# Rotating the odd halves ahead of the selection's refinements, and laying ScalarE's counts up to band step 40

## The chip, the cores and the metric

The kernel runs as one program on one core of a Trainium2 chip. The metric is the device time of one execution in microseconds, from a median of several runs. TensorE has two clock levels, 1.2 and 2.4 GHz; the profile prints the granted clock as a share of the higher one.

## What is computed

One post-norm decoder layer on 1024 tokens of width 1024, in float32. The part that matters here is the first: one input projection feeds two head groups. Group A scores all earlier keys with an indexer, keeps the 256 best keys of each query and attends to these; group B attends within a window of 128. After it come memory cross-attention and a squared-ReLU MLP.

```
proj = h @ w_in + b_in
dq, dk, dv, iq, ik, iw, sq, sk, sv = split(proj)
dq, dk, iq, ik, sq, sk = apply_rope(each, cos, sin)
score = sum_heads iw * relu(iq . ik) * idx_scale        # -inf above the diagonal
sel = top_k(score, 256)                                 # per query
o_dsa = softmax(dq . k[sel] / 8) @ v[sel]
o_swa = softmax([sq . sk / 8 within 128 keys, sink]) @ sv
h = layer_norm(ALPHA * h + concat(o_dsa, o_swa) @ w_o)
h = layer_norm(ALPHA * h + memory_cross_attention(h, mem))
h = layer_norm(ALPHA * h + squared_relu_mlp(h))
```

## The kernel before, in words

Every float32 product is made of three fp32r matmuls (high times high, low times high, high times low: lines 872 to 874). Whoever makes an operand therefore rounds it to a high part and subtracts to get a low part.

**Projection and rotation.** TensorE works through 28 halves `v` (14 units `r`, two halves each; `project`), 24 matmuls of 512 columns a half, in two PSUM banks by turns. A half may start when VectorE has read the bank of the half two before. For the even half VectorE does `rope_first` (lines 1689, 1691), for the odd half `rope_second` (1706 to 1716). Then ScalarE rounds both rows (`round_roped`, 1276) and stores them to HBM (`store_roped`), GpSimd makes the low parts (774) and ScalarE stores these too (`store_low`).

**Selection.** The 256th best score of each query is found by bisection over the bits of a float, for the six query tiles 2 to 7 (numbered `c` = 0 to 5). A count is one pass over a tile's scores with a trial value. Narrow tiles are counted on VectorE (`tally`, 1787), in `select_for`, which takes steps of a generator (`select_keys`) until a budget of estimated microseconds is used up. Wide tiles are counted on ScalarE (`count_scores`, 1305, a Sign with an accumulator): four tiles per half beside the halves from v = 18 on (`BESIDE_HALF`), then three tiles (5, 4 and 3, widths 1024, 896 and 768) in 63 late counts, spread evenly over the band steps from `COUNT_FROM` to `COUNT_TO`. For each count VectorE issues a find (1763, waits for the count) and an apply (1771, sets the next trial, for which ScalarE's next count of that tile waits). `set_all` puts these pairs on a list `pending`; each step of `select_for` takes one entry off it, `flush(k)` takes entries off until k are left.

ScalarE's order beside the halves is: four counts of the even half, the stores of the last unit's low parts, four counts of the odd half, then the two roundings and their stores. VectorE's order is that of the loop over `v` in its block (shown in the diff).

**Entry to the band.** Before half 27 ends, ScalarE rounds the memory tokens (`round_mem`, 1339) behind the four counts of half 26; VectorE subtracts (`split_mem`, 1972); TensorE's first memory product waits for that.

**Band.** 40 steps `n`, one for each pair of heads of ten tiles (eight of the window, and the first two of sparse attention, which need no selection). A step has TensorE's scores (926, 927), VectorE's mask (2018), ScalarE's two exponentials (1403), TensorE's transposes (1014), ScalarE's copy of them (1414), TensorE's product with the values (1034). Beside them TensorE does the memory cross-attention's weight products (`memory_product`): per memory head four pieces of key and value products with nothing to copy out but two roundings, then eight absorbed products, each of which ScalarE copies out (`stage_out`, 1376) and stores before TensorE may use the bank again. GpSimd splits their weights (782, 787).

**Sparse attention** of the other six tiles follows (steps 40 to 87). A tile's first mask (2035) stands behind the end of its selection on VectorE (`select_until`). The selection's part for the three wide tiles starts when the last of the 63 counts is applied (`wide_set`).

Lines that the prediction's steps touch:

```
COUNT_FROM, COUNT_TO = 3, 32                                        # 198
lo, hi = (left * (m - COUNT_FROM) // (COUNT_TO - COUNT_FROM) for m in (n, n + 1))
NARROW_EARLY, BUDGET_BAND = 0.9, 2.1
```

Of the kernel before, what the change touches and what calls it, by code (L numbers as in the profile page):

```python
# [123 lines left out]
def index_carried(v):  # L124

    return index_rows(v)[0:3] if v % 2 == 0 else range(0)


def index_own(v):

    return index_rows(v)[len(index_carried(v)):]
# [63 lines left out]
N_EARLY_COUNTS = len(COUNTS)  # L195
COUNTS += [(c, k) for k in range(LAST_EARLY_BIT - 1, -1, -1) for c in WIDE_TILES]
BEFORE = [max((p for p in range(q) if COUNTS[p][0] == COUNTS[q][0]), default=None) for q in range(len(COUNTS))]
COUNT_FROM, COUNT_TO = 3, 32


def counts_beside_rope(v):

    if v < WIDE_HALF:
        return range(0)
    n = len(EARLY_TILES)
    return range(n * (v - WIDE_HALF), n * (v - WIDE_HALF + 1))
# [11 lines left out]
NARROW_EARLY, BUDGET_BAND = 0.9, 2.1  # L218
# [81 lines left out]
def build_layer(nc, a):  # L300
# [6 lines left out]
    with ctx:  # L307
# [1305 lines left out]
        def _(dve):  # L1613
# [62 lines left out]
            def rope_first(r):  # L1676

                n, s = A_ROPE + 2 * r, r % 2
                what, hf = ROPE[r][1:]
                tok = slice(hf * HALF, (hf + 1) * HALF)  # L1680
                b = bias_qk[:, BIAS_COLUMN[what]:BIAS_COLUMN[what] + 1]
                if r == 0:
                    dve.wait_ge(trig_done, 2)
                if r >= 2:

                    dve.wait_ge(qk_stored[s], 64 * (r // 2))
                filled(dve, a_full, n)
                src = ring_a[n % 2][:]
                then(dve.scalar_tensor_tensor(out=roped[s][0][:], in0=src, scalar=b, in1=cos[:, tok],
                                              op0=ALU.add, op1=ALU.mult))  # L1690
                dve.scalar_tensor_tensor(out=roped[s][1][:], in0=src, scalar=b, in1=sin[:, tok],  # L1691
                                         op0=ALU.add, op1=ALU.mult).then_inc(a_free[n % 2], 1)

            def rope_second(r):

                n, s = A_ROPE + 2 * r + 1, r % 2
                what, hf = ROPE[r][1:]
                tok = slice(hf * HALF, (hf + 1) * HALF)
                b = bias_qk[:, BIAS_COLUMN[what] + 1:BIAS_COLUMN[what] + 2]
                filled(dve, a_full, n)  # L1700
                src = ring_a[n % 2][:]
                turned = swa_out if r in ROT_IN_PSUM else rot_part[:]
                if r:

                    dve.wait_ge(rope_done, 2 * r)
                c1 = then(dve.scalar_tensor_tensor(out=turned, in0=src, scalar=b, in1=sin[:, tok],
                                                   op0=ALU.add, op1=ALU.mult))
                dve.wait_ge(dve_step, c1)
                emptied(dve, a_free, n - 1)
                dve.tensor_tensor(roped[s][0][:], roped[s][0][:], turned, ALU.subtract)\  # L1710
                    .then_inc(rope_done, 1)
                dve.wait_ge(rope_done, 2 * r + 1)
                dve.scalar_tensor_tensor(out=turned, in0=src, scalar=b, in1=cos[:, tok],
                                         op0=ALU.add, op1=ALU.mult).then_inc(a_free[n % 2], 1)
                emptied(dve, a_free, n)
                dve.tensor_tensor(roped[s][1][:], roped[s][1][:], turned, ALU.add).then_inc(rope_done, 1)
# [8 lines left out]
            def rotate_and_split(v):  # L1725

                r, h = divmod(v, 2)
                for n in index_own(v):
                    index_sum(n)
                if h == 0:  # L1730
                    rope_first(r)
                    return
                carried = index_carried(v + 1)
                rope_second(r)
                for part in range(2):
                    for n in carried[part:part + 1]:
                        index_sum(n)
                    if r < POOL_SPLIT:
                        split_roped(r, part)
                for n in carried[2:]:  # L1740
                    index_sum(n)

            def index_sum(n):

                i, h = IDX[n]
                width = (i + 1) * P
                dve.wait_ge(relu_done, n + 1)
                src, w = ring_i[n % 3][:, 0:width], v_all[:, i, h:h + 1]
                if h == 0:
                    dve.tensor_scalar(score[i][:], src, w, None, ALU.mult).then_inc(i_free[n % 3], 1)  # L1750
                else:

                    indexed(dve, i_free, n - 1)
                    dve.scalar_tensor_tensor(out=score[i][:], in0=src, scalar=w, in1=score[i][:],  # L1754
                                             op0=ALU.mult, op1=ALU.add).then_inc(i_free[n % 3], 1)
                if h == HEADS - 1:
                    indexed(dve, i_free, n)
                    own = slice(i * P, width)
                    chain(dve.tensor_tensor(score[i][:, own], score[i][:, own], causal[:, P:2 * P], ALU.add))
# [175 lines left out]
            def set_all(counts):  # L1935

                for q in counts:
                    pending.extend(set_counted(q))
# [6 lines left out]
            def select_for(us, carry=False):  # L1945

                credit[0] = us + (credit[0] if carry else 0.0)
                while credit[0] > 0 and len(selected) < NT:
                    cost, tile = next(selection)
                    if cost is None:  # L1950
                        credit[0] = 0.0
                        return
                    credit[0] -= cost
                    if tile is not None:
                        selected.add(tile)
                    if pending:
                        pending.pop(0)()

            def flush(left=0):
                while len(pending) > left:  # L1960
                    pending.pop(0)()
# [101 lines left out]
            for v in range(last_half):  # L2063
                if v - 1 in INDEX_HALVES:
                    prepare(INDEX_HALVES[v - 1] - FIRST_TOPK_TILE)
                if v >= BESIDE_HALF:

                    set_all(counts_beside_rope(v))
                    if v % 2:
                        flush(2)  # L2070
                        select_for(NARROW_EARLY)
                        flush()
                    else:
                        select_for(NARROW_EARLY)
                        flush(2)
                rotate_and_split(v)
                flush()
            split_mem()
# [380 lines left out]
```

## Time and profile before

| | us |
|---|---|
| median of 3 runs | 1544.46 (1541.53 to 1545.77) |
| the profiled execution | 1540.02 |
| its span, first to last instruction | 1538.1 |
| TensorE matmul busy | 1457.1 (95% of the span) |
| VectorE busy | 1092.8 (71%) |
| GpSimd busy | 757.8 (49%) |
| ScalarE busy | 497.8 (32%) |

Shares are means over stages with different limits: the projections end at about 247 us, the band runs from there to about 431 us, sparse attention to about 557 us, then output projection, cross-attention and the MLP, which fill the rest. Times of rows are microseconds from the start of the span. In rows of the timeline the first number is the start, the second the duration; what stands in brackets is how long the engine had been idle before and whose end it had waited for. PE is TensorE, PEld its weight loads, DVE VectorE, ACT ScalarE, POOL GpSimd.

### The profile page before, as it was taken

What the parts mean: (1) busy time and instruction counts of PE and PEld (TensorE: products, weight loads), DVE (VectorE), ACT (ScalarE), POOL (GpSimd) and SP (SyncE); (2) the same over time, 40 slices, a digit from 0 to 9 for tenths busy, and PEclk for the clock granted to TensorE, in tenths of its full rate; (3) what the DMA queues carried; (4) which work ended last, traced back from release to release, by engine and by line L of the source; (5) the groups of instructions that cost most, each with busy time, mean ns of one, the idle gap of its engine ahead of it and who ended that gap; (6) DMA issues with size and microseconds to landing.
All of it is one profiled execution on the core that took longest, in us unless ns stands there. A gap on an engine that the chain in (4) does not pass through costs nothing.

```text
span 1538.1 us, 21058 instructions
## 1 busy us (share of the span) xinstructions
PE 1457.1 (95%) x7552; PEld 1239.0 (81%) x7552; DVE 1092.8 (71%) x2097; ACT 497.8 (32%) x1044; POOL 757.8 (49%) x583
## 2 busy tenths in 40 slices
PE   6999888898999999989999899999999999999997
PEld 6877667788989988778887688888888888888885
DVE  7568978788888422873517768777777777777857
ACT  3025467889676631122201111111111111111111
POOL 5341348566730032144223357867677777777612
PEclk9999999999999999999999999999999999999999
DMA  6446244565520032221011002011111102020202
GB/s 238 135 160 171 83 166 153 173 188 162 175 69 15 1 133 75 94 83 40 18 53 55 28 28 82 28 55 55 55 55 56 55 28 83 28 82 1 82 28 82
DMA packets 61478, 128.98 MB, mean 84 GB/s; under 512 B 6976, under 2 KB 34112, under 8 KB 53696
## 3 DMA queue, kind: packets, MB, share of 16 engines
q1 hardware_dynamic: 44352, 100.37, 19.5%
q10 hardware_dynamic: 17024, 27.27, 5.1%
q8 instruction: 61, 1.00, 0.3%
q14 instruction: 41, 0.34, 0.1%
HBM read 100.35 MB, written 27.26 MB: 83 GB/s over the span
## 4 chain that ended last, share of the span: by engine, by line
PE 76%; DVE 13%; issue 5%; ACT 4%; DMA 1%; POOL 1%; ACTq 1%; SPq 0%; DVEq 0%; POOLq 0%
PE banks L872 21%; PE banks L874 21%; PE banks L873 21%; PE banks L1078 4%; PE banks L926 2%; PE banks L1065 2%; PE banks L927 2%; DVE h_buf L2127 2%; PE banks L1034 1%; PE banks L1087 1%; DVE bn L2113 1%; DVE act_lo L2106 1%; DVE score L1754 1%; ACT unread_early L1305 1%; ACT unread_late L1305 1%
## 5 line engine op out<-in xcount | busy, mean ns | idle before, releaser
L782 POOL TENSOR_SCALAR w_hi<-raw 128x512 fp32r<-128x512 f32 x156 | 105.1, 700 | 427.0 <-PE banks L874 282.0
L2252 DVE TENSOR_TENSOR h_buf<-h_buf,banks 128x512 f32<-128x512 f32 x320 | 202.7, 680 | 13.2 <-PE banks L874 9.7
L787 POOL TENSOR_TENSOR w_lo<-raw,w_hi 128x512 fp32r<-128x512 f32 x156 | 210.3, 1380 | 0.0
L872 PE MATMUL banks<-act_hi,w_hi 128*128 128x512 f32 x512 | 200.0, 391 | 1.6 <-DVE act_lo L2106 1.6
L874 PE MATMUL banks<-act_hi,w_lo 128*128 128x512 f32 x512 | 199.7, 390 | 0.0
L873 PE MATMUL banks<-act_lo,w_hi 128*128 128x512 f32 x512 | 199.7, 390 | 0.0
L872 PE MATMUL banks<-seven_hi,hid_hi 128*128 128x512 f32 x392 | 152.6, 389 | 0.0
L872 PE MATMUL banks<-w_hi,act_hi 128*128 128x512 f32 x384 | 152.6, 397 | 0.0
L874 PE MATMUL banks<-seven_hi,hid_lo 128*128 128x512 f32 x392 | 152.5, 389 | 0.0
L873 PE MATMUL banks<-seven_lo,hid_hi 128*128 128x512 f32 x392 | 152.5, 389 | 0.0
L874 PE MATMUL banks<-w_hi,act_lo 128*128 128x512 f32 x384 | 150.0, 391 | 0.0
L873 PE MATMUL banks<-w_lo,act_hi 128*128 128x512 f32 x384 | 149.9, 390 | 0.0
L2215 DVE TENSOR_TENSOR hidden<-hidden 128x512 f32<-128x512 f32 x56 | 53.9, 964 | 119.9 <-ACT hidden L1545 119.9
L1559 ACT ACTIVATE hid_hi<-hidden_sum 128x512 fp32r<-128x512 f32 x70 | 40.4, 625 | 254.7 <-DVE hidden_sum L2223 254.7
L872 PEld LDWEIGHTS banks<-act_hi,w_hi 128*128 128x128 f32 x512 | 96.5, 188 | 22.1 <-issue 2.0
L873 PEld LDWEIGHTS banks<-act_lo,w_hi 128*128 128x128 f32 x512 | 96.5, 189 | 20.0
L874 PEld LDWEIGHTS banks<-act_hi,w_lo 128*128 128x128 f32 x512 | 96.4, 188 | 20.0
L872 PE MATMUL banks<-x_hi,w_hi 128*128 128x512 f32 x224 | 89.6, 400 | 12.0 <-DVE roped L1691 5.0
L1545 ACT ACTIVATE hidden<-banks 128x512 f32<-128x512 f32 x56 | 33.4, 596 | 199.1 <-PE banks L874 199.1
L926 PE MATMUL banks<-key_hi,q_tile 128*128 128x512 f32 (+3 forms) x240 | 85.4, 364 | 10.1 <-DVE score L1750 7.7
L837 POOL TENSOR_TENSOR seven_lo<-seven_sum,seven_hi 128x1024 fp32r<-128x1024 f32 x35 | 88.0, 2514 | 2.9
L787 POOL TENSOR_TENSOR w_lo<-raw_up,w_hi 128x512 fp32r<-128x512 f32 x56 | 88.7, 1609 | 0.0
(222 smaller groups left out, 3511.8 us busy)
## 6 DMA issues: line engine op xcount, KB each, us to landing
raw<-w_down_dram SPq DMA_DIRECT2D x16, 1024.0 KB, 4.8
raw_up<-w_up_dram SPq DMA_DIRECT2D x14, 1024.0 KB, 4.8
q_tile<-qk_dram SPq DMA_DIRECT2D x176, 64.0 KB, 2.8
qk_dram<-q_hi ACTq DMA_DIRECT2D x28, 256.0 KB, 2.1
qk_dram<-roped ACTq DMA_DIRECT2D x28, 256.0 KB, 2.3
x_raw<-x_t_dram SPq DMA_DIRECT2D x8, 512.0 KB, 8.3
raw<-wk_mem_dram SPq DMA_DIRECT2D x4, 1024.0 KB, 6.3
raw<-wv_mem_dram SPq DMA_DIRECT2D x4, 1024.0 KB, 5.5
```

What stands on the lines that cost most here:

```text
L782: pool.tensor_scalar(w_hi[s][:, col], source[:, col], 1.0, 1.0, ALU.mult, ALU.mult)\
L787: pool.tensor_tensor(w_lo[s][:, col], source[:, col], w_hi[s][:, col].bitcast(F32), ALU.subtract).then_inc(w_ready, 1)
L837: pool.tensor_tensor(seven_lo[s][:], source, seven_hi[s][:].bitcast(F32), ALU.subtract)\
L872: pe.matmul(dst, lh, rh, start=(first and n == 0), stop=False)
L873: pe.matmul(dst, lh, rl, start=False, stop=False)
L874: last = pe.matmul(dst, ll, rh, start=False, stop=(final and n == len(parts) - 1))
L926: pe.matmul(dst[:, lo:hi], q, key_hi[key][:, k0 + lo:k0 + hi], start=True, stop=False)
L1078: mm = pe.matmul(ring_a[m % 2][:, h * HEAD:(h + 1) * HEAD], prob_t[d % 2][:, j * P:(j + 1) * P], v_all[:, j, HEADS:HEADS + HEAD], start=(j ...
L1545: act.activation(hidden[hf, odd][:, j, :], ring_a[n % 2][:], ACT.Relu).then_inc(a_free[n % 2], 1)
L1559: act.activation(hid_hi[x % 2][:, j, :], source, ACT.Copy).then_inc(hidden_rounded, 1)
L2215: dve.tensor_tensor(block, block, block, ALU.mult).then_inc(sq_done, 1)
L2252: ins = dve.tensor_tensor(out, out, ring_m[g % 6][:], ALU.add if way > 0 else ALU.subtract)
```

## The change

In VectorE's loop an odd half from v = 19 on now rotates first (`rotate_and_split`), then takes its counts on the list, refines, and applies all that is left; before it applied three of four counts, refined, applied the rest and then rotated. An even half from v = 18 on rotates right after its refinements, with only as many finds and applies done as the refinements took off the list (two entries); before it applied until two entries were left and then rotated. ScalarE's, TensorE's, GpSimd's and SyncE's orders beside the halves stay. The 63 late counts of ScalarE are laid over band steps 3 to 39 instead of 3 to 31; VectorE's finds and applies for them follow one step behind, as before.

```diff
-COUNT_FROM, COUNT_TO = 3, 32
+COUNT_FROM, COUNT_TO = 3, 40
...
                 if v >= BESIDE_HALF:
 
+                    if v % 2:
+                        rotate_and_split(v)
                     set_all(counts_beside_rope(v))
+                    select_for(NARROW_EARLY)
                     if v % 2:
-                        flush(2)
-                        select_for(NARROW_EARLY)
                         flush()
-                    else:
-                        select_for(NARROW_EARLY)
-                        flush(2)
+                        continue
                 rotate_and_split(v)
                 flush()
             split_mem()
```

## Rows read from the trace of the kernel before

**Rows 1.** Page, part 2: TensorE's busy tenths in 40 slices of 38.45 us.
```profile
PE   6999888898999999989999899999999999999997
```

**Rows 2.** Busy time by stretch, two pairs of halves; columns in the first line.
```profile
core 0: us, PE busy (x) PEld busy (x) DVE busy (x) ACT busy (x) POOL busy (x), PEclk, DMA share, GB/s
205.74:219.35 13.61, 11.41 (x49) 8.85 (x48) 10.56 (x39) 9.16 (x19) 7.21 (x6) 1.00 0.58 174
232.96:246.57 13.61, 11.42 (x49) 8.86 (x48) 10.56 (x39) 9.15 (x19) 7.22 (x6) 1.00 0.43 156
```

**Rows 3.** Timeline, TensorE: first and last restart, last projection matmul, first memory product.
```profile
193.94 0.47 PE L872 MATMUL banks<-x_hi,w_hi 128*128 128x512 f32 x1 [1.60 <-DVE roped L1691]
...
241.27 0.47 PE L872 MATMUL banks<-x_hi,w_hi 128*128 128x512 f32 x1 [1.06 <-DVE banks L1713]
...
246.59 0.39 PE L874 MATMUL banks<-x_hi,w_lo 128*128 128x512 f32 x1
...
251.16 0.39 PE L872 MATMUL banks<-mem_hi,w_hi 128*128 128x256 f32 x1 [2.89 <-DVE mem_lo L1972]
```

**Rows 4.** Timeline, VectorE, one pair of halves (24 and 25).
```profile
232.96 0.74 DVE L1689 SCALAR_TENSOR_TENSOR roped<-banks,bias_qk,cos 128x512 f32<-128x512 f32 x1
...
234.27 0.21 DVE L1763 TENSOR_SCALAR refused<-count,offset 128x1 int32<-128x1 f32 x1
...
236.47 0.21 DVE L1763 TENSOR_SCALAR refused<-count,offset 128x1 int32<-128x1 f32 x1 [0.45 <-ACT unread_early L1305]
...
236.85 0.20 DVE L1763 TENSOR_SCALAR refused<-count 128x1 int32<-128x1 f32 x2
...
238.85 0.76 DVE L1706 SCALAR_TENSOR_TENSOR banks<-banks,bias_qk,sin 128x512 f32<-128x512 f32 x1
...
241.76 0.21 DVE L1763 TENSOR_SCALAR refused<-count 128x1 int32<-128x1 f32 x2
```

**Rows 5.** Timeline, ScalarE: rounding, first count of half 26, memory tokens.
```profile
240.36 0.63 ACT L1276 ACTIVATE q_hi<-roped 128x512 fp32r<-128x512 f32 x1 [3.11 <-DVE roped L1710]
...
242.97 1.15 ACT L1305 ACTIVATE unread_early<-score,trial 128x1024 bf16<-128x1024 f32 x1 [0.46 <-ACT q_hi L1276]
...
246.88 1.90 ACT L1339 ACTIVATE mem_hi<-mem_raw 128x2048 fp32r<-128x2048 f32 x1
```

**Rows 6.** Timeline, VectorE: the low part of the memory tokens.
```profile
248.81 2.29 DVE L1972 TENSOR_TENSOR mem_lo<-mem_raw,mem_hi 128x2048 fp32r<-128x2048 f32 x1 [0.47 <-ACT mem_hi L1339]
```

**Rows 7.** Busy time by stretch, the band; columns as in rows 2.
```profile
262.40:400.60 138.20, 122.36 (x927) 115.78 (x926) 110.90 (x512) 122.25 (x299) 89.23 (x97) 0.98 0.57 176
277.80:301.00 23.20, 18.59 (x119) 16.52 (x118) 15.50 (x75) 19.37 (x47) 10.70 (x13) 0.93 0.54 182
301.00:322.30 21.30, 20.26 (x175) 20.05 (x174) 18.29 (x84) 19.83 (x52) 15.91 (x18) 1.00 0.53 151
402.60:430.60 28.00, 25.60 (x192) 23.75 (x191) 26.92 (x70) 14.68 (x45) 20.28 (x22) 1.00 0.61 190
```

**Rows 8.** Groups by line, ScalarE, 251 to 445 us: busy, mean ns | idle before, releasers.
```profile
L1305 ACT ACTIVATE unread_late<-score,trial 128x1024 bf16<-128x1024 f32 (+2 forms) x63 | 65.1, 1034 | 8.3 <-ACT stage_out L1376 4.6 <-DVE trial L1771 3.8
...
L1414 ACT ACTIVATE band_prob_t<-banks 128x512 f32<-128x512 f32 (+1 forms) x40 | 21.9, 548 | 11.6 <-ACT stage_out L1376 8.8 <-PE banks L1014 1.8 <-PE banks L1034 0.9
L1376 ACT ACTIVATE stage_out<-banks 128x512 f32<-128x512 f32 x32 | 18.7, 586 | 6.8 <-DMA g_dram<-stage_out 3.8 <-PE banks L874 3.0
```

**Rows 9.** Timeline, TensorE: three restarts in the band and after.
```profile
292.42 0.47 PE L872 MATMUL banks<-w_hi,kv_hi 128*128 128x512 f32 x1 [2.64 <-issue]
...
424.33 0.47 PE L872 MATMUL banks<-w_hi,kv_hi 128*128 128x512 f32 x1 [1.39 <-issue]
...
557.62 1.16 PE L1087 MATMUL banks<-ident,h_buf 128*128 128x128 f32 x8 [2.35 <-DVE act_lo L2106]
```

**Rows 10.** Timeline, VectorE: last selection step of tile 5, its first mask.
```profile
465.96 0.56 DVE L1874 TENSOR_SCALAR score<-score 128x768 f32<-128x768 f32 x1
...
475.85 0.96 DVE L2035 CUSTOM_DVE_ANT_0 logit<-banks,score 128x768 f32<-128x768 f32 x1
```

## The prediction

> **What bounds the kernel now.** I read the busy tenths first [rows 1]: TensorE is at nine tenths almost everywhere, at eight in slices 5 to 8 and 10 (about 154 to 308 us and 346 to 385 us). The change touches just these: the end of the projections (up to 247 us) and the sliding-window band (251 to 431 us). So the question is who makes TensorE wait in each, stage by stage.
>
> *The rotation half.* One pair of halves takes 13.61 us, and no engine is busy for all of it [rows 2]: it is a chain. TensorE starts each half late, after VectorE has read the bank of two halves before; there are eight such restarts from 193.94 to 241.27 us [rows 3]. VectorE comes late because it waits for ScalarE: before the odd half it applies three counts (the last find, at 236.47, waited for ScalarE), then runs two refinements from 236.85, and only at 238.85 rotates [rows 4]. ScalarE then has idled 3.11 us for that rotation before it may round it, and starts its next counts 2.61 us later [rows 5]. The circle is: rotate, round, eight counts, find, refine, rotate.
>
> *The entry to the band.* After the last projection matmul (246.59) TensorE scores for a moment and then waits 2.89 us for the low part of the memory tokens [rows 3]. That part starts at 248.81 because ScalarE, late by its counts, rounds the high part only at 246.88 [rows 5, 6].
>
> *The band.* From 262.40 to 400.60 us (steps 3 to 32) TensorE is idle for 138.20 - 122.36 = 15.84 us, and ScalarE is busy for 122.25 [rows 7]. ScalarE also stands still behind its own copies before their store is issued: 8.8 + 4.6 = 13.4 us in the band, for 32 copies [rows 8], so 0.42 each and some 10 for the 24 copies of this stretch. That makes 132 of 138: ScalarE is the bound on average. By phase: while key and value products run (301.00 to 322.30) TensorE is idle for only 1.04 us; while the absorbed products with their copies run (277.80 to 301.00) it idles 4.61 [rows 7], as before 292.42, where the bank had not been copied out [rows 9]. The next idle time of TensorE that the timeline marks after 431 us is the one before 557.62 [rows 9]: sparse attention is bound by TensorE, and what the band gains is not taken back there.
>
> **The change, part by part.** *1. The odd half rotates first, the even half waits for one count only.* Nothing is removed: per pair VectorE still has one first rotation (1.31 us, 232.96 to 234.27), one second (2.91, 238.85 to 241.76), two groups of two refinements with a find and apply inside (2.00 each, 236.85 to 238.85) and six more finds with their applies (0.38 each, 236.47 to 236.85) [rows 4]. Sum 1.31 + 2.91 + 4.00 + 2.28 = 10.50 us. ScalarE has eight counts (four take 242.97 to 246.88, 3.91) and two roundings with their stores (240.36 to 242.97, 2.61) [rows 5]: 7.82 + 2.61 = 10.43. TensorE has 48 matmuls; from 241.27 to 246.59 lie 23 steps of 0.231 [rows 3], so 48 make 11.1, or 11.0 without the two slow starts. So each engine has less than 11.1 us of work per pair, and the order must decide whether they overlap.
>
> I walk one pair from the moment T when TensorE fills the odd bank. VectorE rotates to T+2.9, refines to T+4.9, applies three to T+6.05; the next even group refines to T+8.05 and rotates the first half to T+9.35, then applies three to T+10.5. TensorE fills the next odd bank at T+11.0: VectorE waits for it 0.5. TensorE needs the even bank free by T+11.0 (free at T+9.35) and the odd by T+5.5 (free at about T+2.2). ScalarE rounds the second half at T+2.9, may count from T+4.0, and gets its next trial at T+4.9; four counts end at T+8.8, the other four at T+12.7, which the next odd group asks for only from T+15. Nobody waits for ScalarE any more. The added waits: the even group's first find stands ahead of the first rotation; its count ended about T+6.1 and it is asked for at T+7.1. Stores, GpSimd's split (waiting for the rounding) and the weight splits behind it move along with the pair; GpSimd is idle in half of it [rows 2].
>
> So a pair goes from 13.61 to 11.0. TensorE's eight halves from 193.94 take 44 us instead of the 52.9 up to 246.8, and the first restart, held 1.60 us, comes some 0.7 earlier: **-9.6**. At the entry ScalarE finishes its even counts some 2 us ahead of the last matmul and rounds the memory tokens then; the low part (2.29 us) ends about 2.2 us after TensorE's last projection matmul instead of 4.6: **-2.4**. Together **-12.0**. Bounds: -9 if the entry gives nothing and VectorE's slack of 0.5 is lost in half of the pairs; -13 if TensorE's pair takes 10.9 and the entry gap closes.
>
> *2. Counts up to step 40.* The 63 late counts spread over 37 steps instead of 29: 49 stay in steps 3 to 31, 14 go to steps 32 to 39. A count costs ScalarE 1.034 us [rows 8], so 14.5 us leave the saturated stretch. Lower bound of the gain: only what falls on steps with copies, about half, 7. Upper: all 14.5, as TensorE's idle time is 15.84. I take **-10**, between them: the relief in the other half clears ScalarE's backlog before the copies start, but buffers hold only about a step. In steps 32 to 39 (402.60 to 430.60) ScalarE is busy 14.68 of 28.00 us [rows 7]; with 8 standstills of 0.42 some 10 are free, so 14.5 overrun by 4.5. VectorE is busy 26.92 there and gets 14 times 0.38, 5.3 us, into 1.1 of free time: 4.2 over. Behind a find that waits for a late count stand VectorE's next mask, ScalarE's exponential and TensorE's transposes. The two overruns lie side by side, and exponentials run ahead of TensorE; below, the loss is 0, above, 14.5 if each count pushes a copy that TensorE waits for (as at 424.33 [rows 9]). I take **+5**, the nearer to the overruns. The selection ends its part for tile 5 at 465.96 and is needed at 475.85 [rows 10], 9.9 us of cover; a delay of 5 costs nothing, beyond 10 each us would show. Counts now end at step 40, before the selection asks for them some 10 us later.
>
> **Sum:** -12.0 - 10 + 5 = -17.0 us. The profiled execution took 1540.02 us (span 1538.1), the median of the runs is 4.4 us above it, within their spread. 1540.02 - 17.0 = 1523.0 there; on the median, **1527.5**.
>
> **TensorE's clock** is the one place where a rule would alter the sum. The granted clock was 0.93 from 277.80 to 301.00, where it idled 2.64 us before 292.42, and 1.00 from 301.00 to 322.30 [rows 7, 9]. Over 262.40 to 400.60 it was 0.98: 4% of the time, 5.5 us, at 1.2 instead of 2.4 GHz, 2.8 us of work lost. The Trainium skill, "TensorE: Matmul & The Clock Gate" (HAM oscillation), says that an array which stands idle between bursts is throttled again and begins the next burst slowly; by that the shorter idle times would return these 2.8 us as well and the sum would be -19.8, and the trace agrees so far that the slow matmuls follow the longest idle times.
>
> **Rivals.** *A. The late counts eat what the early ones gave.* The early gain is 7, the late loss 12: -7, **1537**. For: VectorE is full in steps 32 to 39; against: ScalarE has 10 us free there. *B. VectorE or ScalarE becomes the bound of the rotations*, by a second circle through the finds, and a pair falls only half way, to 12.3: -5.2 for the pairs, -1.5 at the entry, -5 in the band: -11.7, **1533**. For: 10.50 and 10.43 us of work lie close below 11.0; against: the walk finds no wait. *C. The clock stays up:* -19.8, **1524.7**. *D. The reordering does not do what it says:* TensorE's pair stays at 13.6, since it is held by something that the walk misses; only -5 from the band, **1539.5**. Against: all eight restarts end with a rotation. *E. Slower.* Steps 35 to 39 have copies, counts, finds and the selection's slow last steps at once: each moved count stands before a copy (14.5) and each find before a mask (5.3), in turn, +19.8, while the early relief gives nothing because masks and not ScalarE held TensorE. -12.0 + 19.8 = +7.8, **1552**. It decides once the late loss is over 16.6 with no early gain. Against: the idle times in the copy phases end with copies.
>
> **How the numbers follow.** Forecast 0.61 (its own range 1519 to 1535), A 0.15, B 0.10, C 0.07, D 0.03, E 0.04. The range 1519 to 1538 takes in the forecast, B, C and most of A. About 0.3%, 4.6 us, can be told from no change. Faster by more: forecast, B, C, most of A and half of D, 0.91; same 0.05; slower 0.04.
>
> **What would show it.** Right: no restart with idle time from the third pair on, pairs of 11.0 us, the last projection matmul near 237 us, the wait for the memory tokens at about 1 us, TensorE's idle time between steps 3 and 32 near 6 us instead of 15.84, and steps 32 to 40 about 5 us longer than the 28 here. Wrong: a pair above 12 us with VectorE waiting for a count; steps 32 to 40 longer by 10 or more; masks waiting for the selection near tile 5.

## The result and the profile after

The changed kernel takes **1530.34 us** (median of 4 runs, 1530.00 to 1532.35), the kernel before, on the same chip, 1543.41 (4 runs, 1541.53 to 1545.77): a ratio of 0.9918, interval 0.9905 to 0.9932, or 13.1 us less. The profiled execution of after took 1530.0 us (span 1528.2); that of before 1540.02, below each of its four runs (the prediction took it to lie within their spread), so the two traces differ by only 9.9 us. The forecast was 1527.5.

I follow six events through both traces. Lead is the time by which after is ahead of before.

| event on TensorE | before | after | lead |
|---|---|---|---|
| last projection matmul | 246.59 | 236.59 | 10.0 |
| first memory product | 251.16 | 239.36 | 11.8 |
| transposes of band unit 26 | 384.99 | 363.10 | 21.9 |
| transposes of band unit 33 | 415.45 | 396.06 | 19.4 |
| transposes of band unit 39 | 433.86 | 420.50 | 13.4 |
| end of attention (second group of transposes of `h_buf`) | 557.62 | 545.45 | 12.2 |

**The rotations.** Two consecutive pairs of after, in the columns of [rows 2]:

```profile
207.36:218.40 11.04, 11.04 (x50) 9.17 (x49) 10.54 (x42) 9.22 (x19) 2.89 (x3) 1.00 0.83 248
218.40:229.44 11.04, 11.04 (x50) 9.13 (x50) 10.39 (x40) 9.29 (x19) 10.24 (x11) 1.00 0.70 238
```

A pair takes 11.04 us instead of 13.61, and TensorE is busy for all of it. Of the eight restarts of [rows 3] one is left, and the wait for the memory tokens is shorter (timeline, TensorE):

```profile
193.19 0.47 PE L872 MATMUL banks<-x_hi,w_hi 128*128 128x512 f32 x1 [0.82 <-DVE roped L1691]
...
236.59 0.39 PE L874 MATMUL banks<-x_hi,w_lo 128*128 128x512 f32 x1
...
239.36 0.39 PE L872 MATMUL banks<-mem_hi,w_hi 128*128 128x256 f32 x1 [1.09 <-DVE mem_lo L1972]
```

VectorE's order in a pair (timeline) shows why: the second rotation now waits for TensorE and for nothing else, where in [rows 4] it stood behind a count and two refinements.

```profile
212.56 0.75 DVE L1689 SCALAR_TENSOR_TENSOR roped<-banks,bias_qk,cos 128x512 f32<-128x512 f32 x1
...
214.62 0.20 DVE L1763 TENSOR_SCALAR refused<-count,offset 128x1 int32<-128x1 f32 x1
...
215.26 0.76 DVE L1706 SCALAR_TENSOR_TENSOR banks<-banks,bias_qk,sin 128x512 f32<-128x512 f32 x1 [0.18 <-PE banks L874]
```

**The band.** Busy time from the mask of unit 3 to that of unit 32, and from there to that of unit 39; columns as in [rows 2]. First before, then after:

```profile
262.38:398.89 136.51, 120.67 (x913) 114.09 (x912) 109.21 (x506) 120.56 (x295) 87.54 (x96) 0.97 0.57 179
398.89:427.04 28.15, 26.42 (x207) 25.11 (x206) 27.18 (x76) 15.30 (x47) 21.82 (x21) 1.00 0.52 160
```

```profile
249.87:379.51 129.64, 118.77 (x917) 113.19 (x916) 103.77 (x480) 108.68 (x269) 90.11 (x101) 0.99 0.61 193
379.51:411.05 31.54, 29.60 (x219) 28.17 (x217) 29.62 (x93) 25.50 (x68) 21.95 (x22) 0.95 0.50 154
```

In the long stretch ScalarE has 11.9 us less to do, and the time falls by 6.9. In the short one ScalarE has 10.2 us more and VectorE 2.4, the time grows by 3.4, and VectorE is busy for 29.62 of 31.54 us. The granted clock there is 0.95, before it was 1.00: TensorE ran a part of these steps at 1.2 instead of 2.4 GHz. Its waits at the end of the band, and the transposes of units 38 and 39 (timeline, TensorE):

```profile
398.39 0.66 PE L1034 MATMUL banks<-v_all,band_prob_t 128*128 128x64 f32 x4 [1.94 <-DVE h_buf L2056]
...
411.97 0.41 PE L926 MATMUL banks<-key_hi,q_tile 128*128 128x384 f32 x1 [0.65 <-DVE neg_max L2018]
...
417.30 1.06 PE L1014 MATMUL banks<-ident,band_prob 128*128 128x128 f32 x4
...
420.50 1.06 PE L1014 MATMUL banks<-ident,band_prob 128*128 128x128 f32 x4
```

The transposes of each of these two units took 1.06 us, in before 0.60: TensorE is at half the clock, behind the waits. Just ahead of them stands a third wait, of 2.51 us before 415.50, for `band_prob_t`; ScalarE has a count and a copy in front of it (timeline, ScalarE):

```profile
412.70 1.03 ACT L1305 ACTIVATE unread_late<-score,trial 128x896 bf16<-128x896 f32 x1
...
413.73 0.57 ACT L1376 ACTIVATE stage_out<-banks 128x512 f32<-128x512 f32 x1
...
414.76 0.60 ACT L1414 ACTIVATE band_prob_t<-banks 128x512 f32<-128x512 f32 x1 [0.46 <-ACT stage_out L1376]
```

**Behind the band** the lead stays near 12 to the end of attention. Then 1.6 us go in the next stage, in which the clock was 0.98 (before: 1.00), although TensorE waited 2.36 us ahead of it in after and 2.35 in before:

```profile
545.45:615.07 69.62, 68.09 (x320) 56.51 (x321) 24.00 (x39) 9.59 (x17) 29.40 (x32) 0.98 0.40 136
```

So: rotations -11.8, counts -7.6 up to unit 33 and +7.2 from there to the end of attention, -12.2 in all; then +1.6 from the clock and 0.7 in small pieces up to the span's 9.9.

### The profile page after: what moved, and what is told of

Read it like the earlier page. It is cut to its first block, busy times and chain, and to the rows that moved or that the text cites. A ratio compares the mean times of both kernels' runs of the same rounds, so it can differ in the third digit from the quotient of the medians.

```text
span 1528.2 us, 21072 instructions
## 1 busy us (share of the span) xinstructions
PE 1458.5 (95%) x7552; PEld 1243.1 (81%) x7552; DVE 1088.0 (71%) x2097; ACT 497.6 (33%) x1044; POOL 756.9 (50%) x583
## 4 chain that ended last, share of the span: by engine, by line
PE 80%; DVE 12%; issue 2%; ACT 2%; DMA 2%; POOL 1%; ACTq 0%; SPq 0%; DVEq 0%; POOLq 0%
PE banks L872 22%; PE banks L874 22%; PE banks L873 22%; PE banks L1078 4%; PE banks L926 2%; PE banks L927 2%; PE banks L1065 2%; DVE h_buf L2126 2%; PE banks L1034 1%; PE banks L1087 1%; DVE bn L2112 1%; DVE act_lo L2105 1%; DMA u_dram<-stage_out 1%; DVE score L1754 1%; DVE h_buf L2135 1%
## 5 line engine op out<-in xcount | busy, mean ns | idle before, releaser
L874 PEld LDWEIGHTS banks<-act_hi,w_lo 128*128 128x128 f32 x512 | 96.6, 189 | 20.1
```

What stands on the lines that cost most here:

```text
L874: last = pe.matmul(dst, ll, rh, start=False, stop=(final and n == len(parts) - 1))
```

## Experiments

In the profiles of kernels that are alike up to there the first memory product comes between 237.4 and 240.7 us, by what lies ahead of the first restart. "Net" therefore means a lead less the lead at the first memory product: what the band itself gained. It still scatters, since each kernel has one profile. In seven profiles whose band is the same up to step 32 (after, counts to 40 only, each half alone, and three rows of the table: less selection late, late counts light, both of these) the net at unit 33 is 3.8 to 8.6, so a difference of 4 us there shows nothing by itself. The loss from unit 33 to 39 is steadier: 5.8 to 6.8 in the four of them that are the same to the end of the band.

| kernel | net at unit 33 | net at unit 39 | median us | ratio to before (interval) |
|---|---|---|---|---|
| after | 7.6 | 1.6 | 1530.3 | 0.9918 (0.9905 to 0.9932) |
| new order only | 1.4 | 1.6 | 1530.0 | 0.9902 (0.9885 to 0.9920) |
| counts to 40 only | 7.2 | 0.4 | 1542.9 | 0.9993 (0.9981 to 1.0005) |
| counts to 35 | 2.3 | -1.4 | 1528.1 | 0.9900 (0.9882 to 0.9917) |
| counts by phase | -7.4 | -11.0 | 1538.2 | 0.9955 (0.9938 to 0.9973) |
| less selection late | 8.6 | 2.8 | 1530.3 | 0.9923 (0.9904 to 0.9943) |
| late counts light | 3.8 | -0.6 | 1531.6 | 0.9930 (0.9909 to 0.9952) |
| both of these | 7.1 | 5.8 | 1525.5 | 0.9899 (0.9873 to 0.9925) |
| counts to 37, less selection late | 6.4 | 6.6 | 1524.1 | 0.9878 (0.9860 to 0.9896) |
| the same, more selection early | 2.8 | 1.8 | 1527.5 | 0.9900 (0.9882 to 0.9918) |
| counts to 32, less selection late | 0.5 | -0.4 | 1531.0 | 0.9911 (0.9891 to 0.9932) |

### Which half carries the circle

The odd half's edit alone (the even half is put back by the added line):

```
                     if v % 2:
                         flush()
                         continue
+                    flush(2)
                 rotate_and_split(v)
```

> After, with the even half put back: it waits again for all but two steps of its finds before the first rotation; the odd half still rotates first. Theory (the circle ran through the odd half's rotation, the even half's wait has slack: the walk found its count ready 1 us ahead): pairs of 11.0 to 11.2 us, the first memory product within 0.5 us of after's 239.36. Rival (both halves carry the circle, each about half): pairs of about 12.3, the first memory product near 244 to 246.

The first restart has 1.59 us of idle time as in before; after it comes no other, and the first memory product is at 240.07, 0.2 us outside the expected 0.5. From restart to memory product it is 46.19 us, in after 46.17, in before 57.22. The one run of this kernel took 1533.1 us.

The even half's edit alone:

```
                     set_all(counts_beside_rope(v))
                     if v % 2:
                         flush(2)
                     select_for(NARROW_EARLY)
                     if v % 2:
                         flush()
                 rotate_and_split(v)
                 flush()
```

> After, with the odd half put back: it applies its counts and runs its refinements ahead of the second rotation; the even half selects first and waits for one count less. Theory: the circle is untouched, pairs of 13.4 to 13.7 us, the first memory product near 250 to 251. Rival (both halves carry the circle): pairs of about 12.3, near 245.

Timeline, TensorE, of this kernel:

```profile
228.67 0.47 PE L872 MATMUL banks<-x_hi,w_hi 128*128 128x512 f32 x1 [2.38 <-DVE banks L1713]
...
242.29 0.47 PE L872 MATMUL banks<-x_hi,w_hi 128*128 128x512 f32 x1 [2.41 <-DVE banks L1713]
...
252.17 0.58 PE L872 MATMUL banks<-mem_hi,w_hi 128*128 128x256 f32 x1 [2.91 <-DVE mem_lo L1972]
```

A pair still takes 13.62 us, and the one run took 1545.6. The two waits of about 1.1 of before have become one of 2.4, at the odd half's rotation. So the odd half's order is the change; the even half's is worth the 0.8 us at the first restart.

### The order alone, the counts alone

```
-COUNT_FROM, COUNT_TO = 3, 40
+COUNT_FROM, COUNT_TO = 3, 32
```

> The new order of the odd and even halves alone; the counts end at step 32 as in the kernel before. Theory (the whole gain of the change is the rotations', the two count terms cancel in the band): 11.8 us less than the kernel before, the saving that the trace of after shows at the first memory product (239.36 against 251.16), so about 1531.6, the time of after. Rival 1 (the prediction's own terms: -12.0, and the longer count range worth -5): 1531.4 here and after about 5 faster. As the terms of the range cannot be told apart by this time alone, the second test is the transposes: by the theory the lead over the kernel before stays near 12 us from step 3 to step 39, by rival 2 (the shorter rotation by itself relieves ScalarE in the band) the lead grows past 15 before step 30 with no late counts at all, and the time falls below 1529.

The lead over before stays between 11.4 and 12.4 us from unit 5 to unit 39. The shorter rotations relieve nobody in the band; rival 2 falls. The time is that of after. It is 14.5 us below before where the traces show 12; the interval reaches down to 12.4, and the clock may have a part in it (below).

The old order with `COUNT_TO = 40`:

> The old order of the halves; the counts run to step 40. Theory (early gain and late loss cancel): within 2 us of the kernel before, 1541.5 to 1545.5; the transposes lead the kernel before by 7 to 10 us around steps 26 to 33 and by less than 3 at the end of the band. Rival (the prediction's terms, -10 early and +5 late, hold by themselves and the loss in after came from a clock that fell there by accident): 1538.4, and the lead at the end of the band is 5.

The lead was 6.1 at unit 26, 5.8 at 33 and -1.0 at 39 (7 to 10 early was expected; the net is 7.2, since its memory product came 1.4 us later than that of before); the interval of the ratio holds 1. **The longer range of counts is worth nothing that the times can tell, by itself or in after.**

### Where the late loss comes from

`COUNT_TO = 35`:

> After, with the counts ended at step 35, ahead of the last head's copies. 14 counts left steps 3 to 31 in after, 6 of 63 leave them here. Theory (the late loss of 7.2 us comes from counts beside copies in steps 35 to 39): early gain 6/14 of the 7.6 to 10 that after had by step 33, so 3 to 4, no late loss: 11.8 + 3.5 less than the kernel before, about 1528, 2 to 3 faster than after. Rival (each count costs its time wherever it stands, the early gain was ScalarE's total and is lost again anyway): the same as after, 1530.5. Third way (counts in steps 32 to 34 already push the copies behind them): slower than after, 1532 or more.

The time, 1528.1, is where the theory put it, but its interval overlaps that of after, and the trace speaks against the theory's reason: of the profile's lead of 14.0 at unit 33 only 10.3 is left at unit 39, though no count is set after step 34. (The profiled execution, 1532.8, was the slowest of its five.) So counts beside the copies of steps 35 to 39 are not the whole of it. In steps 32 to 39 VectorE was busy for 29.35 of 30.41 us.

Next VectorE's selection work was cut there:

```
-select_for(BUDGET_BAND if n < NS else ...
+select_for((BUDGET_BAND if n < 33 else 1.2) if n < NS else ...
```

> After, with VectorE's budget of selection work cut from 2.1 to 1.2 us a step from step 33 on: VectorE gets 7 times 0.9 = 6.3 us less there, which it does later in sparse attention; ScalarE's counts stay. In the run with the new order alone the lead over the kernel before is 12.1 us from the first to the last step, in after it is 19.4 at step 33 and 13.4 at step 39. Theory (VectorE, busy for 29.7 of 31.5 us in steps 32 to 39 of after, is what the late counts overload): the lead stays above 17 to the end of the band, and sparse attention hides the rest, about 1526 or 4 less than after. Rival 1 (ScalarE, busy for 28.6 of 31.5 us there, is what they overload): the lead falls to 13 to 14 as in after and the time is 1530. Rival 2 (the selection is late for its first tiles of sparse attention): the band is shorter and the waits come back behind it as masks, 1530 or more.

```profile
379.77:406.98 27.21, 26.19 (x205) 24.80 (x203) 22.54 (x82) 22.82 (x63) 21.39 (x21) 1.00 0.54 165
...
414.80 0.45 PE L1034 MATMUL banks<-v_all,band_prob_t 128*128 128x64 f32 x1 [3.33 <-ACT band_prob_t L1414]
```

(busy time by stretch, units 32 to 39; timeline, TensorE.) VectorE is free, TensorE's wait for `h_buf` is gone, the clock stays at 1.00, and the lead is 18.5 at unit 37. Then one wait of 3.33 us, behind a count and a copy of ScalarE, and the slower clock behind it (transposes of 1.06 us) take it back to 13.4.

Then ScalarE's part was cut instead:

```
+w = P if q >= len(COUNTS) - 14 else (i + 1) * P
-act.activation(discard[:, 0:(i + 1) * P], score[i][:], ACT.Sign,
+act.activation(discard[:, 0:w], score[i][:, 0:w], ACT.Sign,
```

> After, with the last 14 counts (steps 32 to 39) reading 128 columns instead of the tile's 768 to 1024, which leaves part of these counts out: ScalarE has some 14 times 0.7 = 10 us less there, VectorE's finds stay. Theory (VectorE): the lead over the kernel before still falls from 19 to 13 or 15 in steps 33 to 39, the time within 2 us of after. Rival (ScalarE's counts ahead of the copies): the lead stays near 19 and the time falls to 1525.

```profile
381.26:412.51 31.25, 29.33 (x217) 27.91 (x216) 29.62 (x93) 19.96 (x73) 21.83 (x22) 0.95 0.55 162
...
416.53 0.32 PE L1034 MATMUL banks<-v_all,band_prob_t 128*128 128x64 f32 x1 [2.08 <-DVE h_buf L2057]
```

ScalarE is busy for 19.96 of 31.25 us, 5.5 less than in after, and most of the loss is there all the same (4.4 us from unit 33 to 39, in after 6.0), now with waits that end with VectorE: 1.92 us before 400.11, and the one shown. The light counts took 0.40 us each, and ScalarE stood still before them for 5.3 us in all until VectorE had set their trial values.

Both at once:

> After, with both reliefs of the last steps at once: the last 14 counts read 128 columns (which leaves part of these counts out), and VectorE's budget of selection work is 1.2 us a step from step 33 on. Each relief alone left the lead over the kernel before at 13.2 to 13.4 us at step 39, as in after: in the one run the waits ended with ScalarE's band_prob_t (3.33 us), in the other with VectorE's h_buf (1.92 and 2.08). Theory (ScalarE and VectorE are overloaded side by side, and either alone costs the whole loss): the lead stays at 17 to 19 up to step 39, the time is 1525 to 1527. Rival (a third thing, such as the key and value weights of the last head or the masks of sparse attention, holds the last steps): the lead falls to 13 to 14 again, 1530.

```profile
381.31:408.95 27.64, 25.97 (x205) 24.73 (x203) 22.82 (x82) 17.39 (x65) 21.80 (x21) 1.00 0.53 163
...
414.44 0.29 PE L1034 MATMUL banks<-v_all,band_prob_t 128*128 128x64 f32 x1 [1.97 <-ACT band_prob_t L1415]
```

Of the loss of some 6 us 1.3 is left, and the time falls to 1525.5: its four runs (1524.1 to 1529.9) lie below those of after, though the intervals of the ratios overlap. **VectorE and ScalarE are overloaded side by side, and each alone costs TensorE most of the loss**: relieving one shows nothing in the time. Most of what the double relief saves is not waiting, though. From unit 33 to 39 TensorE was idle for 5.10 us in after, 5.54 and 4.51 with one relief, 3.87 with both, and 2.65 in before; the granted clock of this stretch was 0.84, 0.87, 0.88, then 1.00 with both and in before. Both reliefs take away half of the added waiting and all of the slow clock. The lead at unit 33 was 17.6 here, inside the expected 17 to 19; at unit 39 it was 16.3, a little below.

### A version that beats both

`COUNT_TO = 37`, and 1.4 instead of 2.1 us of selection a step from step 33 on:

> A whole kernel built on the reading that both engines are full in steps 32 to 39: after, with the counts ended at step 37 and VectorE's budget of selection work cut from 2.1 to 1.4 us a step from step 33 on. Theory: a lead of 17 to 18 at step 33 (10 of after's 14 counts have left steps 3 to 31, so some three quarters of its 7), still 16 or more at step 39, and the selection, later by about 4 us, inside its 9.9 us of cover: about 1527, 3 less than after. Rival (either engine alone still costs the whole loss): 1530.

```profile
248.18:378.66 130.48, 119.27 (x917) 112.97 (x916) 105.40 (x488) 112.62 (x278) 90.11 (x101) 0.99 0.60 190
378.66:406.99 28.33, 26.67 (x207) 25.18 (x206) 22.81 (x83) 23.26 (x65) 22.12 (x21) 1.00 0.56 169
```

The late steps take 28.33 us, as before the change, with the clock at 1.00. The lead is 20.1 at unit 39 and 20.1 at the end of attention, 13.5 of it from ahead of the band. 1524.1 us: 17.9 below before, and its interval lies below that of after.

Is it the smaller late budget alone? The same with `COUNT_TO = 32`:

> The run with counts to step 37 and less selection late measured 1524.1. Here the counts end at step 32, as in the kernel before and in the run with the new order alone (1530.0); the smaller late budget of selection (1.4 us a step from step 33 on) stays. Theory (the longer range of the counts pays early what the smaller late budget protects; with no late counts the late steps idle TensorE for only 1.5 us in 28): the lead over the kernel before stays at 12 until step 33 and at most 14 at the end, 1528 to 1530. Rival (the smaller budget alone gave that gain, the longer range nothing): 1524 to 1525, with a lead of 17 or more at the end of the band.

1531.0, and no net gain in the band: the budget alone gives nothing. The gain needs both, counts that leave steps 3 to 31 and room for them later on both engines. (Counts to step 37 with the whole budget were not run; counts to 35 with it gave 1528.1.)

With 2.3 us of selection a step up to step 32 and 1.3 after:

> As the run with counts to step 37 and less selection late, but VectorE's budget is 2.3 us a step up to step 32 and 1.3 from step 33 on, so that the selection is not later than in after. VectorE waits for TensorE's scores for 17.6 us in steps 3 to 32 of after, so 0.2 us a step has room. Theory: the lead to step 33 is as in that run, the late steps too, about 1526 to 1527. Rival (the earlier refinements stand before masks and finds, and ScalarE's counts wait for them): the lead at step 33 is smaller by 2 or more, 1529 or more.

The time, 3.4 us longer, lies between the two, and no run of one kernel reaches into the other's. The trace is nearer to the rival: the net at unit 33 is 2.8 instead of 6.4 (one profile each), and VectorE is busy for 113.81 of 133.97 us in units 3 to 32 (105.40 of 130.48 without). VectorE's waits in these steps were not free room.

### Counts shared out by phase

```
+COPY_STEPS = {6, 7, 8, 9, 10, 16, 17, 18, 19, 20, 25, 26, 27, 28, 29}
 # COUNT_TO = 35; a step in COPY_STEPS has weight 1, another weight 3
```

> After, with the counts ended at step 35 and shared out by phase: three in a step with key and value products (steps 3 to 5, 11 to 15, 21 to 24, 30 to 34) for one in a step with copies, 48 and 15 of the 63. Theory (ScalarE binds TensorE only while the copies run; what a count costs there is gained in the other steps, where TensorE idled 1.04 us in 21.3): the copy steps lose about 1.1 counts each against after's 1.7, 15 steps by 0.7 counts by 1.03 us = 11 us off the copies, of which half waits elsewhere; with no late loss about 1524, 5 to 7 faster than after. Rival (VectorE's finds and masks bind in the key and value steps, where it gets 1.3 more finds of 0.38 us each step, and the masks come late): no faster than the run with counts to step 35, or slower, and TensorE's idle times in the key and value steps end with band_prob_t or h_buf behind late masks.

```profile
249.22:388.54 139.32, 124.04 (x922) 116.80 (x921) 105.33 (x489) 110.31 (x273) 90.70 (x102) 0.96 0.57 179
...
339.05 0.32 PE L1038 MATMUL banks<-v_before,band_prob_t 128*128 128x64 f32 x1 [3.65 <-ACT band_prob_t L1418]
```

Slower than after by some 6 to 8 us (by ratio, by medians). In the stretch above TensorE is idle for 15.28 us, in after for 10.87, and busy for 5.3 us more at a clock of 0.96 instead of 0.99. The wait shown is for `band_prob_t`, as the rival had it, but not for a late mask or find. ScalarE's copy ahead of it (timeline; the copy of `band_prob_t` follows at 338.40), and the stores issued from 313 to 340 us (KB each, median us from issue to landing):

```profile
337.34 0.60 ACT L1380 ACTIVATE stage_out<-banks 128x512 f32<-128x512 f32 x1 [4.35 <-DMA u_dram<-stage_out]
```

```profile
u_dram<-stage_out ACTq DMA_DIRECT2D x4, 256.0 KB, 6.8
raw<-wq_mem_dram SPq DMA_DIRECT2D x1, 1024.0 KB, 9.7
```

Freed of counts, ScalarE copies out sooner, and the next copy waits 4.35 us for the store of the one two before: these stores took 6.8 us to land beside a load of weights, in the run with the new order alone 2.9 in the same phase. All of ScalarE's waits for a store of `u_dram` in units 3 to 32 make 9.0 us here and 3.2 in after. So what the theory wanted to give the copies went into the stores. And the steps that got three counts had less room than I took them to have: while the key and value products run ScalarE was busy for 19.83 of 21.30 us [rows 7]. Both can be read in before or after; how much of the loss each took was not tried apart.

## Why the prediction was right and where it was not

**Rotations, -12.0: right**, measured -11.8. Pairs 11.04 (11.0 forecast), last projection matmul 236.59 (237), wait for the memory tokens 1.09 (1.0), none of the restarts behind the first (forecast: none from the third pair on). The parts shift a little: 10.0 for the pairs instead of 9.6, 1.8 at the entry instead of 2.4. The walk had also said that VectorE would wait 0.5 us for TensorE in a pair; it waits 0.18 at 215.26 and 0.33 in the next pair. The odd half's move is what opens the circle, and the run with it alone shows it. This part is no luck: from the first restart to the memory product the 11 profiles with the odd half moved take 46.2 us each, and the two with the old order 57.2 and 57.3.

**Counts in steps 3 to 31, -10: the mechanism right, the size off**, -7.6 at unit 33 (within the bounds of 7 and 14.5; 3.8 to 8.6 in the seven profiles named above, so below 10 in all). ScalarE lost 11.9 us of work; the stretch got 6.9 shorter, and 0.7 came ahead of it. TensorE's idle time fell from 15.84 to 10.87 us (129.64 less 118.77), not to 6; the other 1.9 us are busy time, with the clock at 0.99 instead of 0.97. What the prediction left out is who else TensorE waited for. First TensorE's waits before, units 3 to 32, then those of after, units 3 to 39 (what waits, for what, us in total, times, longest), and ScalarE's copies of after from the groups by line:

```profile
PE banks L872 <- issue: 7.0, 6, 2.6
PE banks L872 <- POOL w_lo L787: 5.1, 4, 1.5
PE banks L1034 <- ACT band_prob_t L1414: 3.0, 3, 2.3
PE banks L872 <- ACT stage_out L1376: 0.8, 1, 0.8
```

```profile
PE banks L872 <- issue: 4.8, 5, 1.7
PE banks L872 <- POOL w_lo L787: 2.9, 3, 1.4
PE banks L1034 <- DVE h_buf L2056: 1.9, 1, 1.9
PE banks L872 <- ACT stage_out L1376: 1.8, 1, 1.8
PE banks L1034 <- ACT band_prob_t L1414: 1.3, 1, 1.3
```

```profile
L1376 ACT ACTIVATE stage_out<-banks 128x512 f32<-128x512 f32 x32 | 18.7, 585 | 4.3 <-DMA u_dram<-stage_out 3.2 <-DMA g_dram<-stage_out 0.9 <-PE banks L874 0.2
```

The waits named "issue" are waits for ScalarE's copies too. The prediction read the one before 292.42 so, and the timeline bears it out. First ScalarE before, then ScalarE and TensorE after:

```profile
290.72 1.03 ACT L1305 ACTIVATE unread_late<-score,trial 128x896 bf16<-128x896 f32 x1
...
291.74 0.57 ACT L1376 ACTIVATE stage_out<-banks 128x512 f32<-128x512 f32 x1
```

```profile
275.33 1.03 ACT L1305 ACTIVATE unread_late<-score,trial 128x896 bf16<-128x896 f32 x1
...
276.36 0.57 ACT L1376 ACTIVATE stage_out<-banks 128x512 f32<-128x512 f32 x1
...
277.03 0.47 PE L872 MATMUL banks<-w_hi,kv_hi 128*128 128x512 f32 x1 [1.72 <-issue]
```

TensorE starts 0.1 us behind the copy's end, and the copy stands behind a count. All six waits of this name before and four of the five after end with a copy; the fifth (0.34 us) ends with VectorE's `kv_lo`. In units 3 to 32 TensorE thus waited for copies for 7.7 us before and 6.2 after, for GpSimd's low parts of the weights (872 <- 787) for 5.1 and 2.9, for `band_prob_t` for 3.0 and 1.3. The 5.1 us for GpSimd were no part of the prediction's account, and the wait for copies fell by only 1.5 us where ScalarE's work shrank by 11.9. Part of the reason is their own stores: in units 3 to 32 the copies waited for a store for 0.5 us before and 4.1 after. One of these waits, of 0.88 us before the copy at 367.49, stands ahead of TensorE's longest wait in units 3 to 32, 1.78 us, behind which the clock is 0.89 from 364 to 380 us and the lead falls from 21.9 at unit 26 to 19.4.

**Counts in steps 32 to 39, +5: mis-sized**, +7.2 to the end of attention. The prediction laid ScalarE's and VectorE's overruns side by side and counted them once; the runs show them so, each enough by itself for most of the loss. What the term left out is the clock. From the transposes of unit 33 to those of unit 39, first before, then after (columns as in [rows 2]):

```profile
415.45:433.86 18.41, 15.76 (x107) 13.87 (x106) 17.80 (x41) 10.81 (x30) 14.29 (x16) 1.00 0.53 174
396.06:420.50 24.44, 19.34 (x107) 17.38 (x106) 21.62 (x63) 19.35 (x50) 16.45 (x17) 0.84 0.42 141
```

TensorE's idle time grows from 2.65 to 5.10 us; the same 107 matmuls take 3.6 us more, at a clock of 0.84 instead of 1.00, and those behind them up to the end of attention another 1.2. So the waits that the two overruns add are 2.5 us, less than the forecast 5, and 4.8 us are the slower clock behind these waits. No run holds the clock apart from the waits. In the run with the new order alone, where units 32 to 39 take 28.16 us, and in the fastest version the clock of these units is 1.00.

**The sum** -17.0 was -12.2 at the end of attention: the two count terms came out as -0.4 together, not -5. That the late counts eat what the early ones gave is what rival A said, with other amounts (early 7, late 12; measured 7.6 and 7.2). So the forecast of the time came out by its first term: with the second at nothing it would have been 1532.5, also inside the range of 1519 to 1538, and that 1527.5 was missed by only 2.8 us owes something to chance. The total by medians, -13.1, is nearer to the forecast than the traces' -9.9, since the profile of before lay below its runs; its mean clock was 0.989, that of 17 runs of this kernel 0.9864.

**Rival C, the clock.** The rule drawn on in the prediction, from the Trainium skill, "TensorE: Matmul & The Clock Gate" (HAM oscillation), agrees with the runs in the main: the granted clock is higher where idle times go and lower where they come (an exception stands in the last section). The mean granted clock of whole runs is 0.9864 for the kernel before (17 runs), 0.9895 with the new order alone (4), 0.9870 in after (4), 0.9850 with the counts to 40 alone (12) and 0.9896 in the fastest version (5). A rough estimate from these: a time multiplied by its clock is what it would be had TensorE run at 2.4 GHz throughout. That makes 1523.4, 1513.4, 1510.9, 1520.1 and 1507.8 us. By it the new order alone takes away 10 us of waiting and gets 5 from the clock; the counts to 40 take away another 2.5 to 3.3, and the clock takes most of that back. A clock is printed to 0.001, which is 1.5 us, and over the 17 runs of before the product scatters as widely as the times (1519.1 to 1526.7), so the 2.5 to 3.3 are an indication and no more; where the clock changed is seen only in the one profiled execution of each kernel. Rival C itself is out: 1530.3, not 1524.7. The clock rose from 0.97 to 0.99 in units 3 to 32, as it said, but fell from 1.00 to 0.84 behind unit 33.

Rivals B, D and E are out: pairs of 11.04, not 12.3 or 13.6, and a faster kernel. The selection's cover for tile 5 was not touched: it ends at 453.78 and is needed at 463.67, 9.9 us as in [rows 10].

Open: how much of the late loss would be left at a steady clock, and why that loss differs by a microsecond or two between kernels that differ little.

## What to carry to other kernels

When one engine's work is spread over more steps, add up every engine that it touches in the steps that receive it (here VectorE had 1 us free of 28, and each count brought it a find and an apply), and list everyone that the bound engine waits for in the steps that are relieved (here GpSimd's weights and ScalarE's copies, which still stood behind counts and stores). Where a row names "issue", look at what the other engines end just before. Two engines that are overloaded in the same steps hide each other, so relieve both before saying that neither is the cause. Where a chain goes round, look for the one instruction whose order closes the circle: the odd half's rotation ahead of two refinements gave nearly the whole of the gain.

## What the runs showed of the hardware

VectorE's smallest operations of the selection (one value a partition, two operands in SBUF) take 0.16 us in some places and more than 1 in others, by what GpSimd does. After, timeline of VectorE, then of GpSimd:

```profile
406.88 1.07 DVE L1898 TENSOR_TENSOR level<-level,plain 128x1 f32<-128x1 f32 x1
407.99 1.20 DVE L1899 SCALAR_TENSOR_TENSOR level<-count,level 128x1 f32<-128x1 f32 x1
409.22 0.21 DVE L1771 TENSOR_SCALAR trial<-refused,trial 128x1 int32<-128x1 int32 x1
409.35 1.09 DVE L1902 TENSOR_TENSOR level<-level,plain 128x1 f32<-128x1 f32 x1
410.48 0.16 DVE L1903 TENSOR_TENSOR threshold<-sign,level 128x1 f32<-128x1 f32 x1
```

```profile
405.39 5.03 POOL L787 TENSOR_TENSOR w_lo<-raw,w_hi 128x512 fp32r<-128x512 f32 x4
```

GpSimd runs four subtractions of 1.26 us each until 410.42. The three slow operations begin inside the second, the third and the fourth, and each ends within 0.04 us of that subtraction's end (about 407.91, 409.17 and 410.42). The operation at 410.48 begins behind the last one and takes 0.16. An apply, at 409.22, which takes its second value as a scalar operand, needs only 0.21 beside the fourth. The Trainium skill, "SBUF — State Buffer" (SBUF: two separate sides), says that VectorE with two SBUF operands and GpSimd share a pair of ports and that the later one stands still until the other's instruction ends; these rows agree. It costs VectorE some 3 us in the fullest steps of the band (an estimate from the rows: what three such operations take above 0.16 us), about the same before and after the change.

The clock does not follow from an idle time's length alone. Behind the waits of 1.94 and 2.51 us at the end of the band TensorE ran at 1.2 GHz for a time; behind a wait of 1.96 us before 411.95, at the same place in the run with the counts to 40 alone, the granted clock stayed at 1.00 (up to 425 us). And ahead of the output projection TensorE waits 2.34 to 2.36 us in every kernel, and the eight transposes behind that wait took 1.16 us in before [rows 9], 1.62 in after and 1.94 in the fastest version.
